# Scratch tiles laid out 32 bytes lower, and another order of the last state-space group in a hybrid encoder layer

## The reference

```python
h = x + 0.5 * swiglu(rmsnorm(x))                       # FFN of width 2816
u = rmsnorm(h)
y_gla = gated_linear_attention(u) @ w_branch_gla       # 4 heads
y_ssm = ssd(conv(u @ w_xbc), ...) @ w_branch_ssm       # 8 groups of 256 channels, 2048 in all
y_att = chunk_attention(u) @ w_branch_attn             # 16 heads
g = sigmoid(u @ w_gates + gate_bias)                   # three gates of width 1024
h = h + (g[0] * y_gla + g[1] * y_ssm + g[2] * y_att) @ w_out
h = h + 0.5 * swiglu(rmsnorm(h))
return rmsnorm(h)
```

## The kernel before

| tiles | before | after |
|---|---|---|
| `UH`, `GH`, `SH` | 17536 = 64 x 274 | the same |
| `UL`, `GL` | 33920 = 64 x 530 | the same |
| `WH`; `WL` | 62592; 74880 (multiples of 64) | the same |
| `ident` | 88608 = 64 x 1384 + 32 | the same |
| `NH`; `NL` | 108192; 124576 (multiples of 64, + 32) | 108160; 124544 (multiples of 64) |
| `HH`; `HL` | 120480; 165536 (+ 32) | 120448; 165504 (multiples of 64) |
| `SL`, `AH`; `AL` | 140960; 157344 (+ 32) | 140928; 157312 (multiples of 64) |
| `MH`; `ML` | 190112; 206496 (+ 32) | 190080; 206464 (multiples of 64) |

## Time and profile before

### The profile page before, as it was taken

One profiled execution on the slowest core, in us unless ns is written; L12 is line 12 of the kernel. 1 busy time (PEld: TensorE's weight loads), 2 busy tenths in 40 slices (PEclk: granted clock), 3 DMA queues, 4 the chain that ended last, 5 costly groups with the idle time before them and its releaser, 6 DMA issues.

```text
span 1848.5 us, 26276 instructions
## 1 busy us (share of the span) xinstructions
PE 1817.7 (98%) x9852; PEld 1499.5 (81%) x9852; DVE 961.3 (52%) x1360; ACT 622.2 (34%) x986; POOL 115.5 (6%) x109
## 2 busy tenths in 40 slices
PE   7999999999999999999999999999999999999997
PEld 5888888887888888788888888887888888888885
DVE  6444443379888888532544445555334544444333
ACT  4323222234444444332233244443222323232221
POOL 4111100001101100000000000000000011111000
PEclk9999999999999999999999999999999999999998
DMA  4332223331222222222222222222232223232331
GB/s 157 100 97 96 98 95 102 102 98 62 70 68 68 79 68 68 80 92 95 88 85 75 82 89 85 84 91 69 92 98 95 91 94 99 94 99 92 109 104 58
DMA packets 47353, 164.92 MB, mean 89 GB/s; under 512 B 5520, under 2 KB 6672, under 8 KB 47296
## 3 DMA queue, kind: packets, MB, share of 16 engines
q1 hardware_dynamic: 43584, 158.10, 26.4%
q10 hardware_dynamic: 3712, 6.03, 1.1%
HBM read 162.01 MB, written 2.10 MB: 89 GB/s over the span
## 4 chain that ended last, share of the span: by engine, by line
PE 75%; issue 19%; DVE 3%; POOL 1%; ACT 1%; DMA 0%; POOLq 0%; DVEq 0%; SPq 0%; ACTq 0%
PE G L536 37%; PE G L578 12%; PE I L536 9%; PE G L552 7%; PE I L898 1%; POOL hid L458 1%; PE I L932 1%; PE I L908 1%; PE I L707 1%; PE I L715 1%; PE G L765 1%; DVE UL L1495 1%; PE I L725 1%; PE I L868 0%; PE I L872 0%
## 5 line engine op out<-in xcount | busy, mean ns | idle before, releaser
L1479 DVE TENSOR_TENSOR WL<-RAW,WH 128x1024 fp32r<-128x1024 f32 x297 | 374.1, 1262 | 309.6 <-ACT WH L1027 300.7
L1027 ACT CAST WH<-RAW 128x1024 fp32r<-128x1024 f32 x297 | 309.3, 1046 | 240.6 <-PE I L536 131.9
L536 PE MATMUL G<-UH,WH 128*128 128x512 f32 x696 | 172.9, 390 | 0.0
L536 PE MATMUL G<-UH,WL 128*128 128x512 f32 x696 | 171.9, 389 | 0.0
L536 PE MATMUL G<-UL,WH 128*128 128x512 f32 x696 | 171.8, 389 | 0.0
L536 PEld LDWEIGHTS G<-UH,WH 128*128 128x128 f32 x696 | 130.6, 188 | 28.0 <-issue 1.0
L536 PEld LDWEIGHTS G<-UL,WH 128*128 128x128 f32 x696 | 130.7, 188 | 27.1
L536 PEld LDWEIGHTS G<-UH,WL 128*128 128x128 f32 x696 | 130.7, 188 | 27.1
L536 PE MATMUL G<-NH,WH 128*128 128x512 f32 x448 | 115.5, 399 | 0.0
L536 PE MATMUL G<-NL,WH 128*128 128x512 f32 x448 | 113.6, 395 | 0.0
L536 PE MATMUL G<-NH,WL 128*128 128x512 f32 x448 | 113.6, 395 | 0.0
(11 more groups left out here) (309 smaller groups left out, 2551.4 us busy)
## 6 DMA issues: line engine op xcount, KB each, us to landing
RAW<-in_slabs SPq DMA_DIRECT2D x297, 512.0 KB, 3.3
h<-in_x SPq DMA_DIRECT2D x4, 512.0 KB, 6.4
bias<-in_rel ACTq DMA_DIRECT2D x16, 128.0 KB, 3.1
out_y<-h ACTq DMA_DIRECT2D x8, 256.0 KB, 2.2
bias<-in_rel ACTq DMA_DIRECT2D x16, 112.0 KB, 2.6
cst<-in_cst SPq DMA_DIRECT2D x1, 168.0 KB, 3.6
ut<-in_wgk SPq DMA_DIRECT2D x3, 32.0 KB, 8.3
```

What stands on the lines that cost most here:

```text
L536: ins = mm(dst, W[:, n.slot, (k - k0) * P:(k - k0 + 1) * P], R[:, k, :], start=begin and which == 0 and k == k0, stop=end and which == 2 a ...
L1027: nc.scalar.copy(WH[:, n.slot, :], RAW[:, n.slot, :]).then_inc(split_hi, 1)
L1479: V.tensor_tensor(WL[:, n.slot, :], RAW[:, n.slot, :], WH[:, n.slot, :].bitcast(F32), ALU.subtract).then_inc(split_lo, 1)
```

## The change

It has two parts. In the allocation, `four_eps` (16 bytes, in a place of 32) goes from the common constants into the state-space stage's scratch, so that all that is allocated behind it starts 32 bytes lower; `PT2`, `mx`, `ngm`, `rs`, `rc` (attention scratch) share the place of `SC`, and `DAH` goes into the preparation scratch, which makes the room. In TensorE's order for group 7, `output_half` of slab n+1 goes between `ssm_turn` and `ssm_cb_u`, `output` of slab n+2 ahead of `ssm_inter` and `ssm_intra`, the first part of slab n+4 ahead of `turn_back`, and slab n+5 is split like slab n+4: six of its k-blocks right behind `turn_back`, the last two at the end. No other engine's order changes.

```diff
-        four_eps = sb("four_eps", [P, TT])
...
         rstd4 = sb("rstd4", [P, TT])
+        late = ExitStack()
+        PT2 = sb("PT2", [P, 2, 256], F32, late)
+        mx = sb("mx", [P, 2, TT], F32, late)
+        ngm = sb("ngm", [P, 2, TT], F32, late)
+        rs = sb("rs", [P, 2, TT], F32, late)
+        rc = sb("rc", [P, 2, TT], F32, late)
+        late.close()
         SC = sb("SC", [P, 32, HS])
...
         dtw = sb("dtw", [P, 6, P], F32, prep)
+        DAH = sb("DAH", [P, TT * HS], F32R, prep)
         prep.close()
...
         after_r = sb("after_r", [P, P], F32R, w)
-        DAH = sb("DAH", [P, TT * HS], F32R, w)
+        four_eps = sb("four_eps", [P, TT], F32, w)
...
             output(n, wn, NH, NL)
             ssm_turn(g)
+            output_half(n + 1, wn + 1, 0)
             ssm_cb_u(g)
-            output_half(n + 1, wn + 1, 0)
+            output(n + 2, wn + 2, NH, NL)
             ssm_inter(g)
             ssm_intra()
-            output(n + 2, wn + 2, NH, NL)
             output_half(n + 3, wn + 3, 0)
-            turn_back(Y, I01, ("ssm_scaled", "ssm_scaled_act"), g, "ssm_turned")
             need_slab(n + 4)
             output_part(n + 4, wn + 1, KT, 2 * KT - 2, SH, SL, False, False)
+            turn_back(Y, I01, ("ssm_scaled", "ssm_scaled_act"), g, "ssm_turned")
+            need_slab(n + 5)
+            output_part(n + 5, wn + 3, KT, 2 * KT - 2, SH, SL, False, False)
...
             output_part(n + 4, wn + 1, 2 * KT - 2, 2 * KT, SH, SL, False, True, KT - 2)
-            output_half(n + 5, wn + 3, 1)
+            output_part(n + 5, wn + 3, 2 * KT - 2, 2 * KT, SH, SL, False, True, KT - 2)
```

More of the change, by code:

```diff
@@ L287, in build @@
         PT = sb("PT", [P, 2, 2 * T], F32, w)
[L288 to L292, removed]
         w.close()
```

## The result

The changed kernel takes 1829.34 us (median of 4 runs, 1828.42 to 1830.17), the kernel before 1852.05 us beside it: ratio 0.9881, 95% interval 0.9868 to 0.9893. That is 22.7 us less; the forecast was 22.8 less, 1830. So the total came out as forecast, and the order of group 7 went as foreseen. The cause given for the larger part was wrong, as the experiments show.

The account below looks back on a forecast made before the run. TensorE, busy 1817.7 of 1848.5 us, was taken as the bound. Shifted tiles (19.7 us less) and group 7's order (3.1 less) summed to 22.8 us less, 1830 us on the scale of the medians; range 1823 to 1838.

Parts of the forecast that it names:

- I take the address as the cause of the 6.6 ns: 512-column matmuls: a moving tile starting off a multiple of 64 bytes costs one 64-byte piece more, 6.6 ns.
- The second rival, the place: Moving tiles: dear because high in memory, not for their address; moving them brings nothing, time 1849.9 us; chance 0.08.
- the slower one: Moving tiles: a multiple of 64 itself costs 1.6 ns more on 5216 matmuls; time 1858.2 us; chance 0.04.
- 3392 matmuls by 6.6 ns: Large products whose moving tile shifts 32 bytes: each matmul saves 6.6 ns, together 22.5 us less.
- part one: Allocation: NH/NL, HH/HL, SL, AH/AL and MH/ML start 32 bytes lower, at multiples of 64; 19.7 us less.
- less the 1.2 covered by waits: Gain lost to waits: 1.0 us at attention's softmax, 0.2 at the NH slab in front of group 0.
- tail: Merges and group 7: unmoved SH terms slow for following an SL term get faster, 1.3 us less.
- token-major pairs: Line 578, with NH/NL stationary: 19 slab pairs get dearer by 0.15 us each, 2.9 us more.
- The wait in front of the transposes: Attention: matmuls covering the softmax shrink by 0.2 us, so TensorE waits that long before transposing PR; 5 times, 1.0 us lost.
- Layout in all: The 32-byte shift of the tiles as a whole: 23.8 us gained, less 2.9, 1.0 and 0.2, giving 19.7.
- The order: Group 7, TensorE's new order: waits of 3.6 us go, 0.5 stays ahead of C times state; 3.1 us less.
- The first rival: Group 7: Y is ready late, TensorE waits 2.4 us at turn_back, the order brings 0.7; 1832.6 us; chance 0.10.

Follow-up runs that it names:

- the early turn: Changed kernel with group 7's turn of Y (8 transposes) put ahead of slab n+4's matmuls instead of behind them; 1834.01 us, ratio 0.9903 to the kernel before.

## Why the prediction was right or wrong

**"I take the address as the cause of the 6.6 ns": wrong.** This is the step that failed, though the total came out. The arithmetic of one 64-byte piece fitted the two rows exactly and was an accident of them. The run with everything 32 bytes further shows it: no tile of the large products on a multiple of 64, same time. What the change did was to bring the moving tiles from 32 to 0 bytes after the stationary ones modulo 256. Since all stationary tiles of these products were on multiples of 64, both theories gave the same forecast. Why the distance counts is not shown. That weights are loaded while the matmul before streams, so that two reads meet, is an idea that fits, since PEld is busy for 82% of the span, and is only argued; no run takes the weight loads away.

**The second rival, the place, and the slower one** both fall: a down matmul is at 226.7 ns, high in memory, not at 233 or over 234, and the lowest tiles become dear when `WH` moves. The slower rival had seen something true: of the distances measured, the token-major product is dearest at 0. But at 11.51 us its price was in the sum.

**3392 matmuls by 6.6 ns: the size held where runs are long.** The times between starts, from the trace of the order alone to that of the changed kernel, against the terms of part one:

| term, us gained | forecast | traces |
|---|---|---|
| `NH/NL` moving, less the 1.2 covered by waits | 10.9 | 9.2 |
| `HH/HL` | 7.0 | 7.0 |
| `SL`, `AH/AL`, `MH/ML` | 3.4 | 3.4 |
| tail: `SH`, `GH`, which did not move | 1.3 | 1.0 |
| token-major pairs | -2.9 | -2.8 |
| all else | 0 | -0.7 |
| sum | 19.7 | 17.1 |

Down product 123.20 to 119.68 us, as forecast (twice 3.5 us over the two FFNs); merge 2's 600 139.28 to 136.00, forecast 136.0; token-major pairs 11.51, forecast 11.5. It was too large where the stretches are short, and these are of `NH`. A round gained 43.69 - 43.32 = 0.37 us and not 0.5. From the first scores of round 1's attention to the last ones, the traces are 0.55 us apart, where my terms gave 336 matmuls by 6.6 ns, 2.2, less three token-major pairs by 0.15 and less 0.8 lost to waits: 1.0. In the attention of the changed kernel:

```profile
1077.19 2.12 PE L554 MATMUL G<-NH,WH 128*128 128x512 f32 x8
...
1079.15 1.99 PE L554 MATMUL G<-NL,WH 128*128 128x512 f32 x8
...
1080.97 1.98 PE L554 MATMUL G<-NH,WL 128*128 128x512 f32 x8
...
1082.79 1.98 PE L554 MATMUL G<-NH,WH 128*128 128x512 f32 x8
...
1084.79 0.86 PEld L912 LDWEIGHTS I<-ident,PR 128*128 128x128 f32 x8 [0.45 <-DVE PR L2019]
1084.80 1.09 PE L912 MATMUL I<-ident,PR 128*128 128x128 f32 x8
```

After small products the first eight take 1.96 us, the second 1.82, the third 1.81. Eight by 226.7 is 1.81; 0.1 of the first 1.96 is the gap between the first two starts, the change from small products, which the kernel before paid too. There the first eight behind the earlier trace rows's 1088.25 took 1.98 and the second 1.86: the first hardly gained. So a stretch of 512-column matmuls that follows small ones begins with some seven to ten at about 232 ns, and only the others are mended; that is why the term with which a slab begins, `NH` by high weights, gained 4.2 ns a matmul in the groups, and `NL` 6.5. I had priced every matmul at the settled value. The wait in front of the transposes came about as forecast: from the last product's start to the first transpose's it is 0.42 us in place of 0.27, so 0.15 more where I had put 0.2.

**The tail of 1.3 us** was right in kind and came to 1.0: the `SH` terms behind an `SL` term were slow because the distance changed at each of them, and are now at 226.7 in merge 1.

**Layout in all: 19.7 us forecast.** By the medians it is 16.9 alone and 1847.9 - 1829.3 = 18.6 on top of the new order, by the traces 16.5 and 17.1. The step that was mis-sized is the settled price for short stretches; the lower clock in group 7 took another 1.7 us when the layout stood alone.

**The order: right.** Forecast 3.1 us, measured 3.3 alone (3.4 by the traces). The wait ahead of C times state is 0.52 us (forecast 0.5), the margin at the turn 1.25 (forecast 1.0), and there is no wait at the loop's first slab. The first rival, a wait of 2.4 us at the turn, fails on the row of the tanh, as argued. What I had not seen is that waits can bring the lower clock with them: on the new layout the order brought 5.0 us by the medians (1834.3 to 1829.3) and 4.1 by the traces, 1.7 of them from state updates back at the full clock.

**Why the total came out at 22.7 all the same.** The traces, on whose scale the forecast of 22.8 was worked out, are 20.1 us apart. The other 2.6 us lie in how the profiled executions stand among the rest: 1850.31 is 1.7 under the median of its kernel, and 1830.17 is 0.8 over that of the changed one, whose first matmul starts 0.7 us later. The kernel before also has executions with a mean granted clock of 0.994, at 1852.1 to 1853.9 us, beside such with 0.996, at 1849.8 to 1850.8. None of the 28 executions of the five kernels that have the new order and were timed several times, without the early turn, is at 0.994, while two of four of the layout alone are. This fits waits in group 7 that in some executions bring the lower clock, a gain of the order that I had not counted. It is not shown: no trace has an execution of the kernel before in which that happens, and the profiled execution of the early turn has 0.994 with a clock of 1.00 in group 7. So the layout was put too high by 2.6 us, and what lies between the profiled executions and the medians made up for it. The closeness to 22.8 is luck.

## What to carry to other kernels

Where TensorE is the bound and weights are loaded beside the products, compare the ns per matmul of runs of one shape across the chain; if they differ, move one tile by a few dozen bytes and look again, since what counted here is where the moving tile starts against the stationary one modulo 256 bytes, and one product's best place may not be another's. Price short stretches from short stretches, not from the settled run. And before a theory of addresses is used for a forecast, look for a run in which it and its neighbour differ: shifting everything by the same amount costs one line.

## What the runs showed of the hardware that was not expected

- The price by distance in the table above. Even at distance 0 a 512-column matmul takes 226.7 ns here. The Trainium skill ("TensorE: Matmul & The Clock Gate", "Wait — 56ns, not 53.3ns?") gives N / 2.4 GHz and about 2.5 ns, 215.7; no run of this study came down to it.
- A 256-column matmul took 113.5 ns with `WH` 64 bytes before `NH` and 119.9 at distance 0, while a 512-column one was cheapest at 0, so the best distance is not the same for the two products.
- After a change of distance, or behind small products, some seven to ten matmuls pass before the price settles (1.86, 1.82, 1.81 us for three times eight).
- Waits of 1.41 and 1.27 us in group 7 were followed by a granted clock of 0.53 for 3.6 us with the layout alone, and by 0.50 (742 to 744 us) with the tiles 32 bytes up; in the trace of the kernel before, with waits of 1.42 and 1.28, it stayed at 1.00, and so it did after the single wait of 2.81 us of the early turn. With the wait of 4.3 us ahead of group 0 it fell in the kernel before (0.74 in 432 to 436 us), and with the one of 6.2 us when half projection n+1 alone was moved. What parts the cases is open.
